# A decoder layer with 32 experts: two VectorE steps of the first expert blocks issued ahead of the list of overflow blocks

## The reference

```python
order = jnp.argsort(eid)            # eid: two experts for each token
counts = jnp.bincount(eid, length=N_EXPERTS)
...
def expert_block(args):
    xb, e = args
    hb = jax.nn.silu(xb @ w_gate[e]) * (xb @ w_up[e])
    return hb @ w_down[e]
...
h = _layer_norm(DEEPNORM_ALPHA * x + feats @ w_o, ln1_g, ln1_b)
return _layer_norm(DEEPNORM_ALPHA * h + _hmoe(h, *moe), ln2_g, ln2_b)
```

## Time and profile before

| | us |
|---|---|
| median of 3 runs | 1676.41 |
| lowest and highest | 1675.98, 1680.26 |
| profiled execution | 1677.62 |
| its span, first to last instruction | 1675.8 |
| TensorE busy | 1373.8 (82%) |
| VectorE busy | 593.4 (35%) |
| ScalarE busy | 281.4 (17%) |
| GpSimd busy | 90.6 (5%) |
| share of the chain that ended last: DMA, TensorE | 39%, 23% |

### The profile page before, as it was taken

One profiled execution on the slowest core, in us unless ns is written; L12 is line 12 of the kernel. 1 busy time (PEld: TensorE's weight loads), 2 busy tenths in 40 slices (PEclk: granted clock), 3 DMA queues, 4 the chain that ended last, 5 costly groups with the idle time before them and its releaser, 6 DMA issues.

```text
span 1675.8 us, 24674 instructions
## 1 busy us (share of the span) xinstructions
PE 1373.8 (82%) x10651; PEld 852.8 (51%) x10651; DVE 593.4 (35%) x1280; ACT 281.4 (17%) x659; POOL 90.6 (5%) x116
## 2 busy tenths in 40 slices
PE   8999999999998999969765778757786586676675
PEld 6888788888865677624322333323332233223231
DVE  2845567677676121465301203012030120120124
ACT  0023211210373010211010011101111011010103
POOL 1220011011321000000000000000000000000000
PEclk9999999999999999989887899888998888787887
DMA  9985486786999995269999999999999999999994
GB/s 347 376 277 197 155 294 219 246 316 216 369 387 407 313 307 246 101 256 413 403 426 425 427 421 427 427 427 426 414 427 427 426 427 427 426 428 426 427 425 190
DMA packets 139923, 591.63 MB, mean 353 GB/s; under 512 B 9201, under 2 KB 98785, under 8 KB 107041
## 3 DMA queue, kind: packets, MB, share of 16 engines
q1 hardware_dynamic: 122480, 497.70, 74.7%
q0 software_dynamic: 10624, 76.21, 11.7%
q10 hardware_dynamic: 6704, 16.08, 2.5%
HBM read 580.93 MB, written 17.45 MB: 357 GB/s over the span
## 4 chain that ended last, share of the span: by engine, by line
DMA 39%; PE 23%; DVE 2%; ACT 1%; issue 1%; POOL 0%; DVEq 0%; SPq 0%
DMA arena<-in_w_up 37%; PE ps L2145 8%; PE ps L2086 7%; PE ps L2163 2%; DMA arena<-in_w_down 2%; PE ps L2114 2%; DMA arena<-in_ln_b 1%; PE ps L2077 1%; PE ps L2120 0%; ACT arena L1625 0%; PE ps L2172 0%; PE ps L2194 0%; PE ps L2073 0%; PE ps L2301 0%; PE ps L2205 0%
## 5 line engine op out<-in xcount | busy, mean ns | idle before, releaser
L2145 PE MATMUL ps<-arena 128*32 128x256 f32 x4352 | 337.7, 480 | 242.5 <-DMA arena<-in_w_up 238.4
L2145 PEld LDWEIGHTS ps<-arena 128*32 128x32 f32 x4352 | 184.5, 137 | 411.2 <-issue 361.3
L683 PE MATMUL ps<-arena 128*128 128x264 f32 x1600 | 365.4, 387 | 0.0
L683 PEld LDWEIGHTS ps<-arena 128*128 128x128 f32 x1600 | 300.5, 190 | 49.1 <-issue 0.9
L1906 DVE TENSOR_TENSOR arena<-arena,ps 64x256 f32<-64x256 f32 x34 | 14.4, 424 | 460.8 <-ACT arena L1629 460.8
L2163 PE MATMUL ps<-arena 128*32 128x512 f32 x1088 | 125.8, 602 | 0.5 <-ACT arena L1633 0.4
L2086 PE MATMUL ps<-arena 128*128 128x264 f32 x512 | 120.3, 394 | 2.0 <-PEq L2364 2.0
L1629 ACT ACTIVATE arena<-ps 64x256 f32<-64x256 f32 x34 | 12.8, 375 | 585.7 <-PE ps L2145 585.7
L2086 PEld LDWEIGHTS ps<-arena 128*128 128x128 f32 x512 | 97.1, 192 | 24.3 <-issue 6.3
L2114 PE MATMUL ps<-arena 128*32 128x512 f32 (+1 forms) x816 | 98.5, 595 | 0.9 <-DVE arena L1858 0.9
L1913 DVE TENSOR_TENSOR arena<-arena,ps 128x512 f32<-128x512 f32 x72 | 49.5, 688 | 134.5 <-PE ps L2172 131.7
(11 more groups left out here) (481 smaller groups left out, 1116.6 us busy)
## 6 DMA issues: line engine op xcount, KB each, us to landing
arena<-in_w_gate SPq DMA_DIRECT2D x60, 2048.0 KB, 30.7
arena<-in_w_up SPq DMA_DIRECT2D x60, 2048.0 KB, 34.1
arena<-in_w_down SPq DMA_DIRECT2D x60, 2048.0 KB, 31.2
arena<-in_w_in SPq DMA_DIRECT2D x50, 1024.0 KB, 9.6
arena<-in_w_o SPq DMA_DIRECT2D x16, 1024.0 KB, 11.0
arena<-in_w_down SPq DMA_DIRECT2D x8, 1024.0 KB, 29.4
arena<-in_w_up SPq DMA_DIRECT2D x8, 1024.0 KB, 31.7
arena<-in_w_gate SPq DMA_DIRECT2D x8, 1024.0 KB, 33.0
```

The lines of the kernel that those rows point to most:

```text
L683: last = pe.matmul(ps[:, n % 2, 0:T], ring[:, slot, k, cols], x[:, k, :], start=(k == 0), stop=(k == KT - 1))
L2145: last = pe.matmul(ps[BS * q:BS * q + BS, 0, 0:CHUNK // 2], xs[:, kk * 4 + i, :], ring[:, s, at:at + CHUNK // 2], start=(k == 0), stop=(k ...
```

## The change

`hidden(0)` and `turned(1)` are taken out of the loop over blocks and are issued on VectorE behind the selection of rows and ahead of the overflow list. ScalarE gets a wait for `c_idx` inside `outputs`, ahead of the copies of block 0; the wait for the same value that stands just ahead of the call remains.

```diff
             def outputs(b, first):
                 act.wait_ge(*down_done(b))
+                if b == 0:
+                    act.wait_ge(S["c_idx"], 1)
                 for n in range(4):
@@
             select(code, N_FIRST * BS, N_FIRST * BS, P - N_FIRST * BS)
 
+            hidden(0)
+            turned(1)
             done.link(v.scalar_tensor_tensor(above, wide, -float(BS), counts, ALU.mult, ALU.add))
@@
-                hidden(b)
-                if b + 1 < NB:
+                if b:
+                    hidden(b)
+                if 0 < b < NB - 1:
                     turned(b + 1)
```

## The result

The changed kernel took 1686.48 us (median of 6 runs, 1685.03 to 1689.53), the kernel before 1676.74 beside it (6 runs). The ratio is 1.0048 with a 95% interval of 1.0033 to 1.0062, so 8.0 us slower (5.5 to 10.4). This ratio, which is used throughout, is an estimate from all the runs and not the ratio of the two medians; those lie 9.7 us apart, inside the same interval. The forecast was 1684.0 in a range of 1679.5 to 1687.0.

The account below looks back on a forecast made before the run. The expert weight stream was taken to bound the kernel; row loads 7.63 us late would grow its hole from 1.6 to 9.2 us, so median 1676.41 + 7.6 = 1684.0 us, range 1679.5 to 1687.0.

Parts of the forecast that it names:

- The bound: Expert weight stream near 426 GB/s sets the end; six pairs last to about 758 us, leaving a 1.6 us hole before.
- What becomes earlier: TensorE's `down(0)` ends at about 740.6 instead of 746.3, a head start of 5.7 us, worth 0.
- What becomes later: VectorE's list waits for silu and TensorE's turn, starting 7.63 us late; GpSimd's row loads begin at 745.7 instead of 738.05.
- The loads: GpSimd's last row load again takes 9.9 us, landing at 759.1, 7.6 us later; emptying queue up to -1.
- The restart: TensorE resumes with `spread(0)` at 759.1 instead of 751.4, at low clock; the clock's rise may differ by a microsecond.
- The sum: Pair seven issued at 766.2, stream's hole grows from 1.6 to 9.2 us, everything behind keeps its distances: 7.6 us later.
- Rival 1: Row loads land sooner as the stream thins, the last in 6.0 us: restart 3.7 us late, 1680.1; chance 0.12.
- rival 2: Row loads before `spread(0)` hardly slowed by the stream: not slower, 1676.4, at most 1.6 us gained; chance 0.03.
- Rival 3: GpSimd's row loads take longer, up to 14.2 us: 11.9 us slower, 1688.3; chance 0.09.
- Rival 4: Stream not dry at 758, so weights in the ring hide the delay: time stays at 1676.4; chance 0.05.
- ScalarE's added wait: Second wait for `c_idx` in ScalarE's outputs of block 0, already satisfied when reached: costs nothing.

Follow-up runs that it names:

- e2: Changed kernel, with the eight row loads issued early into free memory without waiting and the list's first row ahead of `hidden(0)`; ratio 0.9986, 2.3 us faster than before.
- e3: Kernel before, with the eight row loads issued early into the same free memory without waiting; ratio 0.9990, 1.7 us faster than before.
- e1: Kernel before, with only the signal to GpSimd's row loads raised later, behind `hidden(0)` and `turned(1)`; ratio 1.0019, 3.2 us slower than before.
- e4: Changed kernel, with only `hidden(0)` ahead of the list and `turned(1)` back in the loop; ratio 1.0035, 5.9 us slower than before.
- the repeat: The changed kernel timed once more, unaltered, against the kernel before; ratio 1.0043, 7.2 us slower.
- e6: As e2, but GpSimd waits for `c_cum`, so the row loads are issued while no weight is moving; ratio 0.9972, 4.7 us faster than before.
- e7_clock_held: Changed kernel with 40 useless products on TensorE between `down(0)` and `spread(0)`; ratio 1.0105, 17.6 us slower than the kernel before.

## Why the prediction was right

- **The bound.** The stream ran dry where the count of chunks said: six pairs, then nothing. In the windows after, it thins out from 762 us, 30 us after the first pair, as it did before at 758. The hole before was put at 1.6 us; with the window of 467 GB/s ahead of it it is 1.4, which changes nothing in the sum.
- **What becomes earlier.** `down(0)` ends at 740.26 on the old clock; forecast 740.6. Worth nothing, as said: e2 against e3.
- **What becomes later.** The waits were forecast as 2.5 and 3.2 us and are 2.45 and 3.17. The list begins 7.5 us late; forecast 7.63. The first row load is issued at 745.57 on the old clock; forecast 745.7.
- **The loads.** I took 9.9 us for the last one; it took 10.2. The doubt that it would go faster in an emptying queue was not borne out. Why a load takes that long the prediction did not say; it carried the 9.9 over to a stretch with the same stream, and there it held, in e1 and e4 as well, where `spread(0)` began 13.6 and 14.0 us after the first issue. Rows 10 give the least, the median and the most of the eight, not their order; that they grow is borne out by another view, with medians of 6.4 us for the first four and 9.1 for the last four.
- **The restart.** `spread(0)` at 759.25 on the old clock; forecast 759.1. The first quarter of block 1 took 0.4 us more, since the low clock lasted longer (9.61 us for `hidden(1)`, 8.44 before), within the microsecond that I had left for it.
- **The sum.** Forecast +7.6, with a hole of 9.2 us; the seventh pair is 8.2 us later (7.5 from the list, 0.3 from the loads, 0.4 from the restart), the hole 9.7, the time +8.0 by the first reading and +7.2 by the second. That everything behind keeps its distances is not quite so: of a hole 8.3 us larger, 6.9 to 7.7 us are left at the end of the span. The median of 1686.48 lies 2.5 over the forecast of 1684.0, above the range given as likeliest (1682.5 to 1685.5) and 0.5 under the upper bound; the repeat's median is 1684.92. The spread of the stretch ahead of the first pair is larger than these distances, so how near the median came is in part luck, while the shift is not.
- **The rivals.** Rival 1 (6.0 us for the last load) and rival 2 (a load hardly slowed) needed a latency that the last of the eight didn't have; e6 shows that rival 2 would have been right for loads in a quiet queue. Rival 3 would have needed 14 us. Rival 4 fell with the windows.
- **ScalarE's added wait** was taken as nothing. e2, in which the outputs of block 0 are as late, bears that out for the delay; the second wait on its own was not tried.

## What to carry to other kernels

When one engine's queue feeds several others, a step that is moved ahead of a long list also moves its waits ahead of everything the list signals. Look for the smallest and farthest consumer (here eight loads of 2 KB on an idle engine), not only for the one that is to gain. In a kernel whose end is set by a weight stream, count how many transfers can be in flight before the ring is full; that gives the moment at which a gain turns worthless and a delay starts to cost its full length. And small loads that a saturated stream must let through are best issued before the stream starts, or as few DMAs: the first closed the hole here in either order of VectorE's work, the second in the order before, while in the changed order it left 3.4 us of 9.7.

## What the runs showed of the hardware that I had not expected

- Loads of 2 KB took 1.6 to 2.1 us with the DMA engines idle, and 5.5 to 10.2 in the changed kernel, with a full stream of 2 MB loads. The number of DMAs counted more than the bytes: under the stream the last of eight loads of 2 KB landed 13.4 to 14.0 us after the first was issued, the last of two of 8 KB after 7.5 or less, and it made no difference whether GpSimd or ScalarE issued the eight. The number of packets did not order the three: 256 for the eight by GpSimd, 16 for the eight by ScalarE, 64 for the two. Eight loads one behind another are not slow by themselves either: in e2, beside 232 GB/s of other loads, each took 5.2 to 5.8 us. What in the DMA engines makes the wait was not looked into.
- After 17.4 us of products at a granted clock of 1.00 and an idle time of 1.65 us, the clock stayed at 1.00 through `spread(0)` (four products with one row of weights) and was at 1.2 GHz for a part of the next 4 us. With no idle time at all, in e7_clock_held, the same products behind `spread(0)` ran at the high level (1.00 from 776 to 784).
- The stretch ahead of the experts varied by 7.5 us between executions. For an edit of a few us behind it, a reading from a fixed event of the trace is sharper than the whole time.
